# Query, retention and gate projections as seven block products through device memory, retention as a stage of its own

## The reference

```python
n = rms_norm(h, norm1_g[l])
proj = n @ w_in[l]
(q_att, c_kv, q_idx, k_idx, w_idx, r_q, r_k, r_v, r_gate,
 g_att, g_ret) = jnp.split(proj, points, axis=-1)
...
_, sel = lax.top_k(score, n_sel)          # 256 of up to 1024 keys for each token
y_att = att.reshape(B, S, ATT_Q_W) @ w_att_branch[l]
ret = retention_chunkwise(...)            # 4 heads, 8 chunks of 128 tokens, a state from chunk to chunk
ret = group_norm_heads(ret, ret_norm_g[l])
y_ret = (jax.nn.silu(r_gate) * ret) @ w_ret_branch[l]
mixed = jax.nn.sigmoid(g_att) * y_att + jax.nn.sigmoid(g_ret) * y_ret
h = h + mixed @ w_out[l]
h = h + hierarchical_moe(rms_norm(h, norm2_g[l]), ...)
```

## Time and profile before

| quantity | value |
|---|---|
| median of three runs | 1498.24 us |
| the profiled execution | 1497.07 us, span 1495.3 us |
| PE busy | 1423.4 us (95%) |
| DVE busy | 1010.2 us (68%) |
| ACT busy | 793.1 us (53%) |
| POOL busy | 640.5 us (43%) |
| first projection matmul, first attention matmul | 156.13 us, 595.15 us |

### The profile page before, as it was taken

One profiled execution on the slowest core, in us unless ns is written; L12 is line 12 of the kernel. 1 busy time (PEld: TensorE's weight loads), 2 busy tenths in 40 slices (PEclk: granted clock), 3 DMA queues, 4 the chain that ended last, 5 costly groups with the idle time before them and its releaser, 6 DMA issues.

```text
span 1495.3 us, 20127 instructions
## 1 busy us (share of the span) xinstructions
PE 1423.4 (95%) x7094; PEld 1184.3 (79%) x7094; DVE 1010.2 (68%) x1457; ACT 793.1 (53%) x1340; POOL 640.5 (43%) x466
## 2 busy tenths in 40 slices
PE   6999999999999999899999999999998599999995
PEld 6887888987798988667668888887886488888884
DVE  4328999999900006666556647888744799999994
ACT  5247323245513526667644456363345388888884
POOL 3410222453923386110035545555332267765654
PEclk9997999999999999899999999999999599999998
DMA  5240556726284325221043356674345898989995
GB/s 188 71 141 1 149 147 138 211 65 165 62 185 92 85 60 201 81 62 31 15 148 100 98 177 224 200 243 143 114 148 215 305 295 214 311 224 355 277 283 78
DMA packets 113813, 235.60 MB, mean 158 GB/s; under 512 B 12848, under 2 KB 34736, under 8 KB 110512
## 3 DMA queue, kind: packets, MB, share of 16 engines
q1 hardware_dynamic: 91056, 176.89, 36.3%
q0 software_dynamic: 18768, 49.29, 16.2%
q10 hardware_dynamic: 3888, 8.13, 1.5%
HBM read 241.87 MB, written 73.14 MB: 211 GB/s over the span
## 4 chain that ended last, share of the span: by engine, by line
PE 83%; DMA 5%; DVE 4%; ACT 3%; POOL 3%; issue 2%; ACTq 0%; SPq 0%; DVEq 0%; POOLq 0%
PE ps L873 23%; PE ps L874 23%; PE ps L875 23%; PE ps L1153 4%; DMA out<-e_y,dest 4%; PE ps L1143 2%; PE ps L1287 2%; DVE dist L1913 1%; PE ps L1091 1%; PE ps L1104 1%; POOL w_lo L2428 1%; PE ps L1106 1%; POOL ro L2496 1%; DMA xin<-in_x 1%; ACT prob L1594 1%
## 5 line engine op out<-in xcount | busy, mean ns | idle before, releaser
L2428 POOL TENSOR_TENSOR w_lo<-w_raw,w_hi 128x512 fp32r<-128x512 f32 (+1 forms) x216 | 306.8, 1425 | 537.0 <-ACT w_hi L1359 460.2
L1359 ACT CAST w_hi<-w_raw 128x512 fp32r<-128x512 f32 (+1 forms) x216 | 132.2, 616 | 448.7 <-PE ps L875 432.7
L873 PE MATMUL ps<-n_hi,w_hi 128*128 128x512 f32 x640 | 250.7, 392 | 1.9 <-DVE kept L2043 1.9
L873 PE MATMUL ps<-w_hi,n_hi 128*128 128x512 f32 (+2 forms) x704 | 244.7, 348 | 7.5 <-POOL w_lo L2428 5.8
L874 PE MATMUL ps<-n_lo,w_hi 128*128 128x512 f32 x640 | 249.3, 390 | 0.0
L875 PE MATMUL ps<-n_hi,w_lo 128*128 128x512 f32 x640 | 249.1, 389 | 0.0
L874 PE MATMUL ps<-w_lo,n_hi 128*128 128x512 f32 (+2 forms) x704 | 242.9, 345 | 0.0
L875 PE MATMUL ps<-w_hi,n_lo 128*128 128x512 f32 (+2 forms) x704 | 242.5, 344 | 0.0
L2366 DVE TENSOR_TENSOR e_lo<-e_raw,e_hi 128x2048 fp32r<-128x2048 f32 x93 | 213.3, 2295 | 25.1 <-ACT e_hi L1777 24.8
L1777 ACT CAST e_hi<-e_raw 128x2048 fp32r<-128x2048 f32 x93 | 177.8, 1914 | 35.8 <-DMA e_raw<-in_w_up 18.5
L2591 POOL DMA_INDIRECT out<-e_y,dest x62 | 145.0, 2339 | 95.4 <-DMA out<-e_y,dest 69.3
(11 more groups left out here) (290 smaller groups left out, 2556.6 us busy)
## 6 DMA issues: line engine op xcount, KB each, us to landing
e_raw<-in_w_gate SPq DMA_DIRECT2D x64, 512.0 KB
e_raw<-in_w_up SPq DMA_DIRECT2D x64, 512.0 KB
e_raw<-in_w_down SPq DMA_DIRECT2D x32, 1024.0 KB
w_raw<-in_w_in SPq DMA_DIRECT2D x64, 256.0 KB, 2.7
w_raw<-sums_dram SPq DMA_DIRECT2D x64, 256.0 KB, 2.9
a_raw<-att_dram SPq DMA_DIRECT2D x36, 256.0 KB, 3.6
a_raw<-ret_dram SPq DMA_DIRECT2D x36, 256.0 KB, 3.9
sums_dram<-in_w_in SPq DMA_DIRECT2D x8, 1024.0 KB, 10.9
```

Source lines behind the costliest of these rows:

```text
L873: mm(out, a[0], b[0], start=first, stop=False, skip_group_check=skip)
L1359: nc.scalar.copy(w_hi[c % NH][:, :width], split_from(c)[:, :width]).then_inc(hi_ready, 1)
L2428: G.tensor_tensor(w_lo[c % NH][:, :width], split_from(c)[:, :width], w_hi[c % NH][:, :width].bitcast(F32), ALU.subtract).then_inc(lo_ready, 1)
```

## The change

The queries, the retention's q and k, its v and its gate are four groups of 1024 columns. In the kernel before they are eight blocks of full products; now each group is made of seven half products, 28 halves of four chunks in all (`PHALVES`, blocks `proj0` to `proj13`), with their results put together in SBUF and sent to device memory (`proj_dram`). The sums of quarters of `n` are built on DVE at the start (`build_sums`), stored (`turned_dram`), and fetched again chunk by chunk for four of the seven halves of each group: SP loads `t_raw`, ACT casts into the quadrant of `n_hi` that is no longer needed, DVE subtracts into `n_lo`. DVE interleaves its picking of keys with these jobs in portions (`pick(1.5)`). The weight sums of all eight groups come from device memory; two times eight copies are spread over the chunk loop, and the last two groups are copied during the attention. The retention follows as a stage of its own: it reads its inputs back from device memory, and its phases stand among the four halves of `ga` and `gb`, which both now come ahead of the attention. DVE masks the scores, runs the states and normalises for all heads. What `ga` and `gb` leave is stored and fetched back behind the attention (four tiles instead of two), with two of the stored sums of `n`.

```diff
+        PHALVES = [(g, p) for g in range(4) for p in (1, 5, 6, 3, 7, 2, 4)]
+        PROJ = [f"proj{n}" for n in range(len(PHALVES) // 2)]
+        blocks += [(name, "T", []) for name in PROJ]
+        T_OF = {5: 0, 6: 1, 7: 2, 4: 3}
+        T_AT = [c for c in range(NPC) if PHALVES[c // 4][1] in T_OF] + [NPC + k for k in range(4)]
-        ret_order = [("block", "gate0"), ("block", "head0"), ("phase1", 0), ("block", "head1"), ("phase2", 0),
-                     ("phase1", 1), ("block", "q0"), ("turn", 0), ("phase2", 1), ("block", "gate1"), ("turn", 1),
-                     ("block", "head2"), ("phase1", 2), ("block", "head3"), ("phase2", 2), ("phase1", 3),
-                     ("block", "q1"), ("turn", 2), ("phase2", 3), ("first", "ga"), ("turn", 3)]
+        ret_order = [("half", j) for j in range(26)] + [
+            ("phase1", 0), ("half", 26), ("half", 27), ("phase2", 0), ("phase1", 1), ("first", 0),
+            ("phase2", 1), ("phase1", 2), ("turn", 0), ("first", 1), ("phase2", 2), ("phase1", 3), ("turn", 1), ("first", 2),
+            ("q", 0), ("turn", 2), ("phase2", 3), ("first", 3), ("turn", 3)]
...
@@ sync: chunks of the projections, and what follows them
+            for c in range(NPC):
+                if c == 4:
+                    sp.wait_ge(sums_added, 16 * 8)
+                load_chunk(proj_at + c)
+                if c in T_AT:
+                    load_turned_n(T_AT.index(c))
+                if 8 <= c < 24 and c % 2 == 0:
+                    copy_quarter(8 + (c - 8) // 2)
+                if 62 <= c < 78 and c % 2 == 0:
+                    copy_quarter(16 + (c - 62) // 2)
+                if c == 88:
+                    load_head(0)
+                    load_rk(0)
+            for c in range(ga, ga + 4):
+                load_chunk(c)
+            for u in range(64, 68):
+                load_turned_n(u)
+            load_rk(1)
+            sp.wait_ge(t_lo, 68)
+            load_head(1)
+            load_gate(0)
...
+            for i in range(2):
+                sp.wait_ge(first_stored[i], 16 * 8)
             sp.dma_start(cst[:, K_TRI:], w["cst"][:, K_TRI:]).then_inc(rest_in, 16)
+            sp.wait_ge(sums_added, 16 * 24)
+            for n in range(24, 32):
+                copy_quarter(n)
             for t in range(NT):
                 if t + 3 < NT:
                     load_q(t + 3)
...
+            for i in range(2):
+                sp.dma_start(sig[2 * i + 1][:, :, 0:BANK], kept_rows[2 * i]).then_inc(first_in, 16)
+                sp.dma_start(sig[2 * i][:, :, 0:BANK], kept_rows[2 * i + 1]).then_inc(first_in, 16)
+            bk.wait_read(sp, ("lg", STEPS - 1))
+            load_sum(2, 0)
+            load_sum(3, 1)
@@ tensor: one half product
+            def half_product(j):
+                g, p = PHALVES[j]
+                name, b0 = proj_half(j)
+                for k in range(4):
+                    c = proj_at + 4 * j + k
+                    pe.wait_ge(lo_ready, c + 1)
+                    if p in T_OF:
+                        u = T_AT.index(4 * j + k)
+                        pe.wait_ge(t_lo, u + 1)
...
@@ scalar: the retention's rounds
+            for i in range(4):
+                c = ga + 4 * i + NH - 1
+                if i == 3:
+                    out_qT(0, 0)
+                    out_qT(0, 1)
+                    out_turn(2)
+                    out_phase2(3)
+                if i in (1, 2):
+                    out_phase2(i)
+                    out_phase1(i + 1)
+                    out_turn(i - 1)
+                hi(c)
+                out_stats(i)
+                hi(c + 1)
+                silu_gate(i)
+                hi(c + 2)
+                hi(c + 3)
@@ vector
+            def pick(us):
+                while us > 0:
+                    us -= next(picking, us)
+            def turned_n_lo(c):
+                if c not in T_AT:
+                    return
+                u = T_AT.index(c)
+                dve.wait_ge(nhi_done, 16 + u + 1)
+                sub(n_lo[:, u % 4, BANK:2 * BANK], t_raw[u % NTR][:], n_hi[:, u % 4, BANK:2 * BANK].bitcast(F32)).then_inc(t_lo, 1)
+            for c in range(NPC + 1):
+                if c and c % 4 == 0:
+                    add_product(c // 4 - 1)
+                if c == 105:
+                    out_phase1(0)
+                turned_n_lo(c + 3)
+                pick(1.5)
+            out_phase1(1)
+            out_phase2(0)
+            pick(1e9)
+            keep_first(0)
...
+            for i in range(1, 3):
+                out_phase1(i + 1)
+                out_phase2(i)
+                keep_first(i)
             out_qT(0, 0)
             out_qT(0, 1)
+            out_phase2(3)
+            keep_first(3)
```

824 lines of the change are left out of this document (431 added, 393 removed).

## The result

The changed kernel takes 1568.24 us in the median of four runs (1566.55 to 1569.87), the kernel before 1498.12: the ratio is 1.047, with a 95% interval of 1.045 to 1.049. The forecast was 1511, with a range up to 1540; the sign is right, but 13 us more were forecast and 70 were measured. The profiled execution has a span of 1567.7 us, 72.4 more than before.

A forecast was written before the change was run, and what follows sets the result against it. PE was taken to bound the kernel (busy 1423.4 of 1495.3 us). Against 1497.07 us, -49.3 - 6.3 + 21.5 + 29 + 14 + 6 + 1 = +15.9 gave 1513, stated as 1511; range 1474 to 1540.

The forecast's parts named there:

- PE's work: Projections: half products replace eight full blocks, 304.6 us of PE work instead of 353.9, a cut of 49.3 us.
- DVE's pace in the projections: Projections: picking, 64 low parts and additions on DVE end after PE alone would, +21.5 us; bounds nothing to +47.
- some 20: Sign in the projections: PE waits for DVE's `n_lo`, in all some 20 us.
- Copies in the chunk loop: Projections: two times eight copies lead PE by 19 us, the queue falls behind by some 13; nothing, at most 8.
- the unnamed wait: Sign of being wrong: a wait shows that the prediction has not named, in the retention rounds above all.
- The retention stage: Stage behind the projections: waits for head 1, banks, query rows and head 3 cost +29 us; 12 to 40 by the bounds.
- Head 1: Retention stage: its load is issued only behind low part 68, so PE waits 14.5 us; bounds 2 and 20.
- The query rows: Retention stage: tile 0's rows come behind SP's chunk loads and a POOL scaling, 4.5 us.
- That lower clock: Rival, retention stage: clock falls to 0.87, matmuls take 10 to 15 us more; with late head 1, 1530; chance 0.10.
- The attention: Attention: tile 3's query rows wait behind eight 1 MB copies in SP's queue, +14 us; bounds 5 and 17.
- Behind the attention: After the attention: 6 MB go ahead of `m7`'s first chunk, whose low part comes late, +6 us; bounds 0 and 9.
- The start: Kernel start: building the sums on DVE falls into a wait that is a few us short, +1 us, at most 4.

The follow-up runs named there:

- x2_light_sums: Changed kernel with 16 copies and 16 adding copies of the projections cut to 8 rows instead of 512: 1539.0 us, ratio 1.0276.
- x6_light_adds: Changed kernel with only the 16 adding copies of pairs 1 and 2 cut to 8 rows instead of 512, plain copies whole: 1543.3 us.
- x13_head1: Changed kernel with copies spread and a sum fetched later (1521.1 us), plus the last four fetched rows put in the gates' place: 1511.2 us.
- x9_att_spread: Changed kernel with attention copies two behind each of four query row loads, POOL's adding copies behind the rows of tiles 5 and 7: 1554.3 us.
- x3_q3_first: Changed kernel with SP loading the query rows of tile 3 ahead of the attention's eight copies instead of behind them: 1567.2 us.
- x18_rows_later: On a 1508.3 us version combining earlier edits, POOL scales the first query rows behind head 2's powers: 1502.1 us, ratio 1.0017 to the kernel before.

## Why the prediction was wrong

**PE's work: right.** Chunks of half products come 2.72 us apart wherever PE does not wait, and the 49.3 us are saved at full clock.

**DVE's pace in the projections: wrong cause, and over-sized.** The term was +21.5, from 64 x 1.09 us for low parts. They take 0.925 us in the mean; 15 of the 66 take over 1 us, where in the branch stage of the kernel before 26 of 48 did:

```profile
L2020 DVE TENSOR_TENSOR n_lo<-t_raw,n_hi 128x512 fp32r<-128x512 f32 x66 | 61.1, 925 | 26.4 <-ACT n_hi L1598 25.8
```

DVE stands 26.4 us in the group's waits, for casts whose transfer is late: it has slack. With 0.925 for 1.16 the forecast's own sum would have given some +6 and not +21.5 (an estimate), and 6.0 us is what PE waits for `n_lo` in `x2_light_sums`; in the changed kernel it is 7.4, where "some 20" was the sign. So the mechanism exists, at a third of its price.

**Copies in the chunk loop: the failed step.** I set them at "nothing, at most 8" by counting SP's queue. They and the adding copies cost 33 us at the end of the projections, and PE's 25.2 us of waits for `w_lo` are the unnamed wait that the prediction gave as a sign of being wrong. Two things were left out. `adds_at` was not costed at all. In the kernel before, these steps stood a block of eight full chunks apart (44 us), and four such copies landed after 16.8 us in the median (160 to 300 us). The changed order leaves 8 and then 6 chunks of 2.72 us (22 and 16 us) between steps that wait for each other, and the four take 26.4 us in the median, so POOL stands 13.5 us in line ahead of all low parts. Nor was the volume costed: 64 fetched sums of 256 KB came in, in less time, so the DMA share went from 0.52 to 0.85 or more. The adding copies are shown to be needed for the loss (`x6_light_adds`, with all fetched sums in place, is 25 us faster); whether they would cost as much without the fetched sums was not tested.

**The retention stage: mechanism right, price too low.** +29 was forecast, 44.5 measured. Head 1 was forecast at 14.5 and waited 10.5, released by the named transfer; `x13_head1` shows the shared place as its cause. The query rows took 6.3 (forecast 4.5), late banks 3.9 (3.5 behind the picking and 1.5), the two waits at turns 9.3 (5). Not forecast: 2.8 us of a turn that waits for `qT_lo_first`'s bank, and the clock. The stretch of 520 to 660 shows it at 0.84. PE's waits in the stage sum to 32.8 us, and PE works 24 us of it at the lower level, which costs 12.0 more: together 44.8, against 44.5. That lower clock I had as a rival at 0.10, with 10 to 15 us. What is left behind `x13_head1` goes, as I read it, round through ACT's squares, POOL's powers and DVE's normalising: taking ACT's copies out gained nothing, taking a stop of POOL out did. That there is nothing else in this ring is not shown.

**The attention: right.** +14 forecast, +14.7 measured (186.2 us against 171.5 before), the gap at tile 3 at 11.98 us with POOL waiting for `qrow`; the rest is mostly work at the lower clock. `x9_att_spread` takes 13.0 of the 14.7 away. `x3_q3_first` adds what I had not seen: POOL's adding copies stand ahead of the rows of tile 4, so the copies hold two places and not one.

**Behind the attention: right place, under-sized.** +6 forecast, +19.3 measured. The transfers ran as worked out (the sum landed at 868.1, 26.5 us into the stage). I let PE wait for the low part of the weight of `m7`'s first chunk, the ninth; in fact ACT, in order, stops for the sum with the cast of the eighth chunk behind it, and PE stops after seven chunks and restarts from an empty line of buffers, at half clock (stretch 860 to 880: PE busy 7.14 of 20 us, clock 0.66).

```profile
860.00:880.00 20.00, 7.14 (x25) 5.42 (x24) 9.74 (x12) 10.43 (x18) 6.83 (x5) 0.66 0.65 220
```

**The start: under-sized.** +1 forecast, at most 4; 3.6 measured.

**The clock, taken together.** A long gap of PE costs itself and work at the lower level behind it: PE's busy time is 27.3 us over the forecast's, about half of the 56.5 us missed, and 22.6 of it are the clock. The kernel before had few such gaps, so I priced waits at their length alone.

## What to carry to other kernels

When a change makes one engine's work shorter, every step that another engine or queue had spaced by that work is compressed with it: list the instructions that are placed by chunk number, above all on an engine that waits for its own transfers, and recompute the time between each and the one that needs it. Cost the bytes of a stage against its new length, not only the order of a queue; and where an in-order engine stops for a transfer, what is late is whatever stands behind it. Price a gap of PE with the slower work behind it, and when one wait is removed by moving a load, look at what the same copies hold up next.

## What the runs showed of the hardware

Adding copies within device memory are dear neighbours: 16 of them cost 25 us of the changed kernel's time (`x6_light_adds`), 16 plain copies of the same size 4 more (`x2_light_sums`). After a gap of 12 us PE came back with matmuls 0.43 us apart, the level of 1.2 GHz, and returned to 0.23 within 10 us (granted clock 0.54 in 440 to 450 us, 1.00 from 460 on). While the adding copies ran, loads of 256 KB on another queue took 9.8 us instead of 3.0. Some of these kernels also vary more: the kernel before kept within 6.5 us in 17 runs, `x18_rows_later` within 15 in 12. Why is not shown; the changed kernel, with the longest waits for transfers, kept within 3.3 us in its four.
